# Prompt attention of a two-layer streaming encoder on Trainium2: item order, score banks, the bias pass and the place where keys are turned

## The chip, the cores and the metric

The kernel runs on one core of a Trainium2 chip. The metric is the device time of one execution in microseconds (us). Engines are called by the profile's names: PE is TensorE (matrix products; PEld its weight loads), DVE is VectorE, ACT is ScalarE, POOL is GpSimd, SP is the engine that issues most loads. Every engine works through its own list in order and waits on semaphores. PSUM is the memory that TensorE writes to: eight banks of 512 fp32 columns on 128 partitions.

## The reference

One call computes a prompt (1024 tokens of one new stream) and a sample step (16 tokens for each of 8 running streams) through two layers. Layer 0 is an mLSTM mixer and a SwiGLU FFN, layer 1 is differential attention on one shared set of keys and values, and a second FFN. The change lies in layer 1's attention of the prompt:

```
def _diff_block(q, k_all, v_all, q_pos, k_pos, rel_bias, lam):
    s = jnp.einsum('bqhjd,bkhjd->bhjqk', q, k_all).astype(jnp.float32) * (DA_DH ** -0.5)
    bias = rel_bias.astype(jnp.float32)[_t5_bucket(k_pos[None, :] - q_pos[:, None])]
    bias = bias.transpose(2, 0, 1)[None, :, None]
    mask = (k_pos[None, :] // CHUNK) <= (q_pos[:, None] // CHUNK)
    p = jax.nn.softmax(jnp.where(mask, s + bias, -jnp.inf), axis=-1)
    a = p[:, :, 0] - lam * p[:, :, 1]
    return jnp.einsum('bhqk,bkhe->bqhe', a.astype(v_all.dtype), v_all)
```

There are 8 heads. Each has two maps (j = 0, 1) of 64 dimensions and values of 128. The output of a head is normalised by its root mean square over the 128 values, scaled, and goes through the output projection. The new keys and values are outputs of the kernel too, in their natural layout (token by token).

## The kernel before, in words

All activations lie transposed in SBUF: features on partitions, the 1152 tokens (1024 prompt, 128 sample) along the row. F1 holds the queries (head h's two maps on partitions 0 to 63 and 64 to 127), F0 the keys in the same way. A projection runs in units of 128 output columns: 72 products of 128 x 384, with activations and weights each split into a high and a low half. SP loads a unit's weights into WRAW, POOL splits them into WHI and WLO, TensorE multiplies, ACT copies the finished group out of PSUM. The stages in order are: query projection `q_a`, key projection `k_a` (eight units, copied to F0), value projection `v_a` (eight units; each group is copied to VT, turned block by block by TensorE, copied to NSA and stored to the output), prompt attention, sample attention, output projection `out_a`.

Prompt attention is written out by hand as 64 items n. Item n covers query tile i = n // 8 and head h = n % 8, so tiles are outermost, and the number of keys w = 128 (i + 1) grows from 128 to 1024 over the stage. An item's work:

- `scores(n)` on TensorE: for each map the product of the query tile and w keys, in chunks of up to 512 columns. Up to 512 keys a map has two banks by turns; above that (wide items) a map has one pair of banks, and its scores wait until the exponentials of the same map of the item before are done.
- `maximum(n, j)` on DVE: adds the bias to the nearest 256 keys and takes their maximum in one pass (L1274), takes the maximum of the far keys in another (L1276), and joins the two and turns the sign (L1278).
- `exps(n, j)` on ACT: the exponential and its sum, from PSUM to one of two buffer pairs (L1154).
- `combine(n)` on DVE: two reciprocals, the factor, and one pass over w columns that joins the two maps (L1291 to L1297).
- `turn(n)` on TensorE: turns the w columns block by block into banks 4 and 5 (L1050); `copies(n)` on ACT copies them to PTS (L1163).
- `values(n)` on TensorE: the product with the values, two passes for each block of 128 keys, into bank 6 (L1063); `outs(n)` on ACT scales it into F1, and squares it for the norm (L1172, L1173).

TensorE takes, for each n, the scores of item n + 1, the turn of item n - 1 and the values of item n - 2. When a query tile's eight heads are done, POOL makes the reciprocal root (L987, L991), DVE scales the tile (L1301), TensorE turns it in two halves into bank 7 (L1040) and DVE copies it back (L1305). In the same stage the keys are turned for the output: TensorE turns half a tile into bank 7 (L1031), ACT copies it to KNAT (L1182) and issues the store, 18 times in all.

Of the kernel before, what the change touches and what calls it, by code (L numbers as in the profile page):

```python
# [18 lines left out]
ALU = mybir.AluOpType  # L19
# [3 lines left out]
P = 128  # L23
# [112 lines left out]
def build(nc, x_prompt, x_sample, state_C, state_n, state_m, cache_k, cache_v, norm_g, mlstm_w_in,  # L136
# [4 lines left out]
    with ctx, nc.allow_non_contiguous_dma(reason="a few gates, stabilisers and tables of rows"):  # L141
# [133 lines left out]
        PR = [r(f"PR{j}", [P, SEQ]) for j in range(2)]  # L275
        PR2 = [r(f"PRB{j}", [P, SEQ]) for j in range(2)]
        PTS = r("PTS", [P, SEQ // P, P])
        KNAT = r("KNAT", [P, 512])
# [592 lines left out]
        a_pt = sem("a_pt")  # L871
        a_cp = sem("a_cp")
        a_o = sem("a_o")
# [3 lines left out]
        k_tr = sem("k_tr")  # L877
        k_cp = sem("k_cp")
        k_sent = sem("k_sent")
# [22 lines left out]
        PAIRS = [PR, PR2]  # L902
        VSTORED = 16 + 32 * (UNITS["v_m"] + UNITS["v_a"])
# [7 lines left out]
        def key_tile(c):  # L911

            return 0 if c < 2 else NQ if c < 4 else c // 2 - 1

        def key_half(n):

            i, h = n // DH, n % DH
            if i < NQ and h in (0, 2):
                return h // 2 if i == 0 else 2 * i + 2 + h // 2
            if i == 0 and h in (4, 6):  # L920
                return 2 + (h - 4) // 2
            return None
# [22 lines left out]
        def attention_sp(sp):  # L945
            sp.wait_ge(nsv_sent, VSTORED)
            sp.wait_ge(group_ready, G0["out_a"])
            sp.dma_start(VP[:, 0, :], vp[:, 0, :]).then_inc(vp_first, 16)
            sp.dma_start(VP[:, 1:, :], vp[:, 1:, :]).then_inc(vp_landed, 16)
# [33 lines left out]
        def attention_pool(pool):  # L983
            for i in range(NQ):
                pool.wait_ge(a_ev, DH * (i + 1))

                pool.tensor_scalar(MSQ[:, :], SSQ[:, i % 2, :], 1.0 / P, EPS, ALU.mult, ALU.add)  # L987
                pool.drain()
                if i >= 2:
                    pool.wait_ge(a_on, i - 1)  # L990
                pool.tensor_tensor(RSTD[:, i % 2, :], MSQ[:, :], HALF[:, :], ALU.pow).then_inc(a_rstd, 1)  # L991
                pool.drain()

        def attention_pe(pe):
# [12 lines left out]
            def scores(n):  # L1007
                i, h = n // DH, n % DH
                w = (i + 1) * P
                wide = w > 512  # L1010
# [1167 lines left out]
```

## Time and profile before

| | us |
|---|---|
| median of three runs | 3546.78 |
| lowest, highest | 3543.9, 3556.37 |
| span of the profiled execution | 3551.3 |
| TensorE busy in it | 3284.0 (92%) |
| DVE, ACT, POOL busy in it | 1146.1, 726.7, 957.0 |

The span runs from the first instruction to the last one of the profiled execution. No time is given apart from it for that execution; the span lies inside the range of the three runs. The profile's busy time of TensorE counts a product from its start to its modelled end, the way through the array included, so a stretch of short dependent products looks busier than its columns are. Of the span, the prompt's attention covers about 1970 to 2292 us, and the key projection and value projection about 1753 to 1960.

### The profile page before, as it was taken

How to read it: one execution, taken by the hardware profiler on the slowest of the kernel's cores; microseconds unless marked ns; L12 is line 12 of the kernel's file. 1: busy time of each engine (PE TensorE's matmuls, PEld its weight loads, DVE VectorE, ACT ScalarE, POOL GpSimd, SP SyncE). 2: the span in 40 equal slices, each digit the busy share in tenths (PEclk: the TensorE clock that was granted, in tenths of full speed). 3: DMA queues.
4: the chain of work that ended last, by engine and by line, in shares of the span. 5: the costliest groups of instructions: out<-in, count | busy, mean ns of one | idle time of the engine just before them, and what ended most of it. 6: DMA issues, size and time to landing. Idle time of an engine off the chain costs nothing.

```text
span 3551.3 us, 45000 instructions
## 1 busy us (share of the span) xinstructions
PE 3284.0 (92%) x18277; PEld 3075.1 (87%) x18277; DVE 1146.1 (32%) x1777; ACT 726.7 (20%) x1199; POOL 957.0 (27%) x449
## 2 busy tenths in 40 slices
PE   7999987979999999988899789899879999999996
PEld 6999877969999999986899456577869999999995
DVE  5100344152222222234200677522234222222225
ACT  4111342230000000023101566411231000000002
POOL 2323001343333333323333000000243333333332
PEclk8999778989999999998999899977799999999998
DMA  4121202101111111112113210153211111111111
GB/s 146 42 83 54 84 30 94 55 24 42 42 41 41 41 41 41 41 36 77 36 42 91 97 39 22 58 178 115 78 30 32 45 42 41 41 41 41 41 42 54
DMA packets 230817, 200.87 MB, mean 57 GB/s; under 512 B 8577, under 2 KB 193310, under 8 KB 230194
## 3 DMA queue, kind: packets, MB, share of 16 engines
q1 hardware_dynamic: 194402, 147.90, 13.5%
q10 hardware_dynamic: 36304, 51.46, 4.2%
q8 instruction: 74, 1.21, 0.1%
q14 instruction: 37, 0.30, 0.0%
HBM read 166.27 MB, written 33.06 MB: 56 GB/s over the span
## 4 chain that ended last, share of the span: by engine, by line
PE 76%; issue 14%; DVE 4%; ACT 2%; POOL 1%; POOLq 1%; DVEq 1%; DMA 0%; ACTq 0%; SPq 0%
PE PS L1581 22%; PE PS L1587 22%; PE PS L1585 22%; PE PS L1127 2%; PE PS L1094 1%; DVE F L2005 1%; PE PS L1105 1%; PE PS L1128 1%; PE PS L508 1%; PE PS L485 1%; DVE F L2018 1%; DVE XLO L1989 1%; POOLq L1507 0%; PE PS L493 0%; PE PS L1117 0%
## 5 line engine op out<-in xcount | busy, mean ns | idle before, releaser
L1581 PE MATMUL PS<-XHI,WHI 128*128 128x384 f32 x3672 | 845.6, 338 | 62.7 <-DVE XLO L1989 62.4
L1506 POOL TENSOR_TENSOR WHI<-WRAW,ZERO 128x1024 fp32r<-128x1024 f32 x197 | 373.6, 1897 | 1904.9 <-PE PS L1581 1875.3
L1585 PE MATMUL PS<-XLO,WHI 128*128 128x384 f32 x3672 | 838.9, 336 | 0.0
L1587 PE MATMUL PS<-XHI,WLO 128*128 128x384 f32 x3672 | 838.6, 336 | 0.0
L1581 PEld LDWEIGHTS PS<-XHI,WHI 128*128 128x128 f32 x3672 | 656.8, 189 | 73.0 <-issue 56.0
L1585 PEld LDWEIGHTS PS<-XLO,WHI 128*128 128x128 f32 x3672 | 659.7, 189 | 0.0
L1587 PEld LDWEIGHTS PS<-XHI,WLO 128*128 128x128 f32 x3672 | 659.0, 189 | 0.0
L1508 POOL TENSOR_TENSOR WLO<-WRAW,WHI 128x1024 fp32r<-128x1024 f32 x197 | 487.5, 2474 | 28.1
L2048 DVE TENSOR_TENSOR F<-F,PS 128x1152 f32<-128x1152 f32 x176 | 238.2, 1353 | 460.4 <-PE PS L1587 460.4
L2033 DVE TENSOR_TENSOR HF<-PS,SG 128x1152 f32<-128x1152 f32 x44 | 59.7, 1357 | 668.3 <-PE PS L1587 668.3
L1863 ACT ACTIVATE HHI<-HF 128x1152 fp32r<-128x1152 f32 x44 | 51.4, 1169 | 1060.6 <-DVEq L2034 1060.6
L1581 PE MATMUL PS<-HHI,WHI 128*128 128x384 f32 x1056 | 243.5, 338 | 5.3 <-DVE HLO L2036 5.3
L1585 PE MATMUL PS<-HLO,WHI 128*128 128x384 f32 x1056 | 242.8, 338 | 0.0
L1587 PE MATMUL PS<-HHI,WLO 128*128 128x384 f32 x1056 | 242.7, 338 | 0.0
L1581 PEld LDWEIGHTS PS<-HHI,WHI 128*128 128x128 f32 x1056 | 189.7, 188 | 6.7 <-DVE HLO L2036 5.9
L1587 PEld LDWEIGHTS PS<-HHI,WLO 128*128 128x128 f32 x1056 | 190.1, 188 | 0.0
L1585 PEld LDWEIGHTS PS<-HLO,WHI 128*128 128x128 f32 x1056 | 189.9, 188 | 0.0
L2036 DVE TENSOR_TENSOR HLO<-HF,HHI 128x1152 fp32r<-128x1152 f32 x44 | 139.0, 3160 | 56.4 <-ACT HHI L1863 56.4
L1019 PE MATMUL PS<-F,F 64*128 64x512 f32 (+3 forms) x384 | 137.5, 545 | 16.1 <-ACTq L1156 12.9
L1858 ACT ACTIVATE SG<-PS 128x1152 f32<-128x1152 f32 x44 | 49.9, 1135 | 421.4 <-PE PS L1587 421.4
L1019 PEld LDWEIGHTS PS<-F,F 64*128 64x128 f32 x384 | 55.2, 200 | 73.1 <-issue 32.4
L1063 PE MATMUL PS<-VP,PTS 128*128 128x128 f32 x576 | 82.5, 291 | 23.9 <-ACTq L1175 23.9
(284 smaller groups left out, 2737.9 us busy)
## 6 DMA issues: line engine op xcount, KB each, us to landing
WRAW<-in_ffn_w_in_dram SPq DMA_DIRECT2D x88, 512.0 KB, 3.8
WRAW<-in_ffn_w_out_dram SPq DMA_DIRECT2D x44, 512.0 KB, 3.6
KC<-in_cache_k_dram SPq DMA_DIRECT2D x16, 1024.0 KB, 7.0
VC<-in_cache_v_dram SPq DMA_DIRECT2D x16, 1024.0 KB, 5.1
WRAW<-in_mlstm_w_in_dram SPq DMA_DIRECT2D x24, 512.0 KB, 3.8
xs_scratch<-F ACTq DMA_DIRECT2D x2, 4608.0 KB, 13.3
F<-xs_scratch ACTq DMA_DIRECT2D x2, 4608.0 KB, 13.9
WRAW<-in_kv_w_dram SPq DMA_DIRECT2D x16, 512.0 KB, 3.9
```

The lines of the kernel that those rows point to most:

```text
L1019: mm = pe.matmul(sflat(j, wide, n)[:, c:e], F1[64 * j:64 * j + 64, h, tile(i)], F0[64 * j:64 * j + 64, h, c:e], start=True, stop=True)
L1063: mm = pe.matmul(PS[:, 6, 0:P], PTS[:, k, :], VP[:, k, h * P:(h + 1) * P], start=k == 0, stop=k == nk - 1)
L1127: pe.matmul(out, VC[m % 4][:, t, h, :], PTC[:, t, 32 * h:32 * h + 32], start=t == 0, stop=False)
L1506: pool.tensor_tensor(WHI[par][:, :, :], WRAW[par][:, :, :], bc(bc(ZERO[:, 0], KT), P), ALU.add)
L1508: pool.tensor_tensor(WLO[par][:, :, :], WRAW[par][:, :, :], WHI[par][:, :, :].bitcast(F32), ALU.subtract).then_inc(w_split, 1)
L1581: mm = pe.matmul(out[:, c, :], wh, rhs_hi[:, chunk(c)], start=first, stop=False)
L1585: pe.matmul(out[:, c, :], wh, rhs_lo[:, chunk(c)], start=False, stop=False)
L1587: mm = pe.matmul(out[:, c, :], wl, rhs_hi[:, chunk(c)], start=False, stop=last)
L1863: act.activation(HHI[:, t, :].rearrange("p (c t) -> p c t", c=NC), HF[:, :, :], ACT.Copy).then_inc(hh_ready, 1)
L2033: dve.tensor_tensor(HF[:, :, :], G(o), SG[:, :, :], ALU.mult).then_inc(group_free[o % 2], 1)
L2036: dve.tensor_tensor(HLO[:, t, :].rearrange("p (c t) -> p c t", c=NC), HF[:, :, :], HHI[:, t, :].rearrange("p (c t) -> p c t", c=NC).bitcas ...
L2048: dve.tensor_tensor(f, f, G(o), ALU.add).then_inc(group_free[o % 2], 1)
```

## The change

- Heads are outermost: item n is head n // 8 and query tile n % 8, so every head starts with 128 keys and ends with 1024.
- The scores of all items, narrow or wide, go to three pairs of banks by turns (banks 0 to 5), item by item and map by map. Item n + 1 waits, once for both maps, for the exponentials of map 0 of item n and of map 1 of item n - 1; the two maps' chunks alternate in the list.
- Bias and maximum are one DVE pass over all w columns, with the sign turned in it. The bias stands in a row of 1024 columns for each head (BROW, two buffers that POOL fills: zeros, and the near 256 columns of a head). The exponential takes scale -1.
- Turned blocks have one bank (6). Blocks one to four are turned and copied by ACT as before; blocks five to eight are turned into the same bank after that copy and copied by DVE. Outputs go to bank 7, by turns with the turned halves of finished outputs. PTS has two buffers, the first map's exponentials three.
- A head's outputs are scaled by POOL in one pass over 1024 columns, where DVE scaled a tile.
- Keys are turned in the key projection, by the code of the value projection, with one more copy into F0. The 18 half-tile turns, copies and stores leave attention.
- The values of the first head are loaded first, where the first tile's were.

```
-        def sflat(j, wide, n):
-            if wide:
-                return PS[:, 2 * j:2 * j + 2, :].rearrange("p b c -> p (b c)")
-            return PS[:, 2 * j + n % 2, :]
+        def sflat(n, j, w):
+            b = 2 * ((2 * n + j) % 3)
+            return PS[:, b:b + 2, :].rearrange("p b c -> p (b c)")[:, 0:w]
...
         def attention_pool(pool):
+            def bias_rows(h):
+                if h >= 2:
+                    pool.wait_ge(a_m[0], NQ * (h - 1))
+                    pool.wait_ge(a_m[1], NQ * (h - 1))
+                pool.tensor_copy(BROW[h % 2][:, SEQ - NEAR:], BIAS[:, h, :]).then_inc(bias_row, 1)
+            pool.wait_ge(group_ready, G0["out_a"])
+            for j in range(2):
+                pool.memset(BROW[j][:, 0:SEQ - NEAR], 0.0)
+            pool.drain()
+            pool.wait_ge(lam_dve, 1)
+            bias_rows(0)
+            bias_rows(1)
+            for h in range(DH):
+                pool.wait_ge(a_ev, NQ * (h + 1))
...
+                o = F1[:, h, 0:SEQ].rearrange("p (i e) -> p i e", i=NQ)
+                pool.tensor_tensor(o, o, bc(RSTD[:, h % 2, :], P), ALU.mult).then_inc(a_on, 1)
...
             def scores(n):
-                for j in range(2):
-                    back = 1 if wide else 2
-                    if n >= back:
-                        pe.wait_ge(a_e[j], n - back + 1)
-                    for c in range(0, w, 512):
+                if n >= 1:
+                    pe.wait_ge(a_e[0], n)
+                if n >= 2:
+                    pe.wait_ge(a_e[1], n - 1)
+                for c in range(0, w, 512):
+                    e = min(c + 512, w)
+                    for j in range(2):
...
+            def turn(n, second):
+                nk = n % NQ + 1
+                if second:
+                    if not wide(n):
+                        return
+                    pe.wait_ge(a_cp, n + 1)
+                    ks_ = range(4, nk)
+                else:
+                    pe.wait_ge(a_c, n + 1)
+                    if n:
+                        pe.wait_ge(a_cp, n)
+                        pe.wait_ge(a_cpb, wides(n - 1))
+                    ks_ = range(min(nk, 4))
...
             for n in range(NI + 2):
                 if n + 1 < NI:
                     scores(n + 1)
+                if n < NI and out_turn(n) is not None:
+                    pe.wait_ge(a_ev, n - 2)
+                    out_half(out_turn(n))
+                    turned = out_turn(n) + 1
                 if 1 <= n <= NI:
-                    turn(n - 1)
+                    turn(n - 1, False)
                 if n >= 2:
-                    values(n - 2)
+                    values(n - 2, turned)
+                if 1 <= n <= NI:
+                    turn(n - 1, True)
...
             act.wait_ge(nsv_sent, VSTORED)
+            act.wait_ge(w_split, U0["out_a"] + 3)
...
+            exps(0, 0)
             for n in range(NI + 3):
                 if n < NI:
                     exps(n, 1)
                 if n >= 3:
                     outs(n - 3)
+                if 1 <= n <= NI:
+                    copies(n - 1)
+                if n + 1 < NI:
+                    exps(n + 1, 0)
...
             def maximum(n, j):
-                dve.tensor_tensor_reduce(near, near, bias, 1.0, -3e38, ALU.add, ALU.max, stat(n, j))
-                if far:
-                    dve.tensor_reduce(stat(n, 2 + j), s[:, 0:far], AX_X, ALU.max)
+                dve.tensor_tensor_reduce(s, s, BROW[h % 2][:, SEQ - w:], -1.0, 3e38, ALU.add, ALU.min, stat(n, 4 + j))
+                dve.drain().then_inc(a_m[j], 1)
...
-            linear("k_a", 4)
-            values("v_a", UNITS["v_m"])
+            values("k_a", UNITS["v_m"], 4)
+            values("v_a", UNITS["v_m"] + UNITS["k_a"])
```

TensorE's list in attention, before, at two items of 768 keys, one with a half of turned outputs (L1019 scores, L1040 turned outputs, L1050 turn, L1063 values; PR and PRB are the two buffer pairs of exponentials):

```order
L1019 MATMUL PS<-F_49,F_50 128x512 [waits a_e0]
L1019 MATMUL PS<-F_49,F_50 128x256
L1019 MATMUL PS<-F_49,F_50 128x512 [waits a_e1]
L1019 MATMUL PS<-F_49,F_50 128x256
L1040 MATMUL PS<-CST,F_50 128x128 [waits k_cp,a_on]
L1040 MATMUL PS<-CST,F_50 128x128 x3
L1050 MATMUL PS<-CST,PRB_145 128x128 [waits a_cp,a_c]
L1050 MATMUL PS<-CST,PRB_145 128x128 x5
L1063 MATMUL PS<-VP,PTS 128x128 [waits a_ev,a_cp]
L1063 MATMUL PS<-VP,PTS 128x128 x5
```

TensorE's list in attention, after, from the second to the fourth tile's scores of a head, with the wide tiles of the head before among them (L1036 scores, L1066 turn, L1082 values; P is an item's first map's buffer):

```order
L1036 MATMUL PS<-F_49,F_50 128x256 [waits a_e1,a_e0]
L1036 MATMUL PS<-F_49,F_50 128x256
L1066 MATMUL PS<-CST,P_143 128x128 [waits a_cpb,a_cp,a_c]
L1066 MATMUL PS<-CST,P_143 128x128 x3
L1082 MATMUL PS<-VP,PTS_147 128x128 [waits a_ev,o_cp,a_cpb,a_cp]
L1082 MATMUL PS<-VP,PTS_147 128x128 x6
L1066 MATMUL PS<-CST,P_143 128x128 [waits a_cp]
L1066 MATMUL PS<-CST,P_143 128x128 x3
L1036 MATMUL PS<-F_49,F_50 128x384 [waits a_e1,a_e0]
L1036 MATMUL PS<-F_49,F_50 128x384
L1066 MATMUL PS<-CST,P_144 128x128 [waits a_cpb,a_cp,a_c]
```

The two maps' scores now follow one another behind one common wait, the turn is in two parts around the values, and the turn also waits for DVE's copies (`a_cpb`); the scores of narrow tiles stand behind the turns and values of the last head's wide tiles.

DVE's list in attention, before, one step of the tile of 512 keys (two maxima, then the combination of the item before):

```order
L1274 ISA PS,ST<-PS,BIAS 128x256 [waits a_c,a_s0]
L1274 ISA ST 128x1
L1276 TENSOR_REDUCE ST<-PS 128x1
L1278 SCALAR_TENSOR_TENSOR ST<-ST,NEG 128x1
L1274 ISA PS,ST<-PS,BIAS 128x256 [waits a_c,a_s1]
L1274 ISA ST 128x1
L1276 TENSOR_REDUCE ST<-PS 128x1
L1278 SCALAR_TENSOR_TENSOR ST<-ST,NEG 128x1
L1291 RECIPROCAL ST<-ST 128x1 [waits a_ev,a_e1,a_e0]
L1292 RECIPROCAL RL_139<-ST 128x1
L1294 SCALAR_TENSOR_TENSOR ST<-ST,LAM 128x1
L1297 SCALAR_TENSOR_TENSOR PRB_145<-PRB_146,ST,PRB_145 128x512
```

DVE's list in attention, after, at the tile of 896 keys, with a half of turned outputs (L1313), the combination of the item of 768 keys and the copy of the item of 640 keys (L1308):

```order
L1285 ISA PS,ST<-PS,BROW_150 128x896 [waits a_e0,a_s0,bias_row]
L1285 ISA ST 128x1
L1313 TENSOR_SCALAR F_50<-PS,LAM 128x512 [waits o_tr]
L1285 ISA PS,ST<-PS,BROW_150 128x896 [waits a_e1,a_s1,bias_row]
L1285 ISA ST 128x1
L1295 RECIPROCAL ST<-ST 128x1 [waits a_ev,a_e1,a_e0]
L1296 RECIPROCAL RL_139<-ST 128x1
L1298 SCALAR_TENSOR_TENSOR ST<-ST,LAM 128x1
L1301 SCALAR_TENSOR_TENSOR P_144<-P_146,ST,P_144 128x768
L1308 COPY PTS_147<-PS 128x128 [waits a_o,a_ptb]
```

Each map has one pass in place of three instructions, and the copy of turned blocks stands at the end of the step.

## Rows read from the trace of the kernel before

**Rows 1.** Windows: length; busy (count) PE, PEld, DVE, ACT, POOL; clock; DMA share; GB/s.

```profile
1973.00:2010.00 37.00, 25.18 (x102) 17.02 (x102) 24.82 (x127) 24.38 (x93) 1.85 (x2) 0.59 0.30 117
2013.00:2068.00 55.00, 41.37 (x232) 24.82 (x232) 46.59 (x191) 41.73 (x132) 3.67 (x4) 0.97 0.17 58
2068.00:2272.00 204.00, 190.59 (x967) 122.03 (x965) 148.81 (x430) 125.60 (x286) 7.33 (x8) 1.00 0.06 22
```

**Rows 2.** Groups by shape, prompt attention: count, busy, mean ns, idle before.

```profile
L1274 DVE CUSTOM_DVE_ANT_0 PS<-PS,BIAS 128x256 f32<-128x256 f32 x112 | 48.3, 431 | 49.5 <-PE PS L1019 47.7 <-DVE PRB L1297 0.5
L1154 ACT ACTIVATE PR<-PS,ST 128x512 f32<-128x512 f32 x8 | 5.5, 685 | 1.6 <-DVE ST L1278 1.2 <-issue 0.3
L1305 DVE TENSOR_SCALAR F<-PS,LAM 128x512 f32<-128x512 f32 x15 | 11.2, 745 | 1.2 <-PE PS L1040 1.2
L1274 DVE CUSTOM_DVE_ANT_0 PS<-PS,BIAS 128x128 f32<-128x128 f32 x16 | 4.8, 299 | 4.4 <-PE PS L1019 3.8
L1297 DVE SCALAR_TENSOR_TENSOR PR<-PR,ST,PR 128x128 f32<-128x128 f32 x4 | 1.4, 352 | 0.3
```

**Rows 3.** Timeline of a step of 768 keys: start, length, engine, [idle before].

```profile
2150.58 0.89 ACT L1154 ACTIVATE PRB<-PS,ST 128x768 f32<-128x768 f32 x1
2151.64 1.55 PE L1019 MATMUL PS<-F,F 64*128 64x512 f32 x4 [0.38 <-ACTq L1156]
2151.65 0.14 DVE L1274 DVE_READ_ACCUMULATOR2_ANT ST<- 128x1 f32 x1
2153.84 1.50 PE L1063 MATMUL PS<-VP,PTS 128*128 128x128 f32 x12
2154.48 0.16 DVE L1291 RECIPROCAL ST<-ST 128x1 f32<-128x1 f32 x1
2155.07 1.02 DVE L1297 SCALAR_TENSOR_TENSOR PRB<-PRB,ST,PRB 128x768 f32<-128x768 f32 x1
```

**Rows 4.** Timeline, TensorE, scores of an item of 512 keys, both maps.

```profile
2069.09 1.13 PE L1019 MATMUL PS<-F,F 64*128 64x512 f32 x4
```

**Rows 5.** Timeline, ACT and TensorE: last key unit, last value units.

```profile
1853.25 1.13 ACT L1830 ACTIVATE F<-PS 128x1152 f32 x1 [11.35 <-PE PS L1587]
1946.49 1.13 ACT L1838 ACTIVATE RS<-PS 128x1152 f32<-128x1152 f32 x1 [2.84 <-PE PS L1587]
1959.97 1.13 ACT L1838 ACTIVATE RS<-PS 128x1152 f32<-128x1152 f32 x1 [2.85 <-PE PS L1587]
1961.15 1.09 PE L1644 MATMUL PS<-CST,RS 128*128 128x128 f32 x8 [1.22 <-ACT RS L1838]
1963.42 0.33 PE L1649 MATMUL PS<-CST,RS 128*128 128x128 f32 x1 [1.17 <-ACT NSA L1842]
```

**Rows 6.** Timeline, first maximum and the end of prompt attention.

```profile
1973.27 0.30 DVE L1274 CUSTOM_DVE_ANT_0 PS<-PS,BIAS 128x128 f32<-128x128 f32 x1
2286.40 0.20 POOL L987 TENSOR_SCALAR MSQ<-SSQ 128x8 f32<-128x8 f32 x1 [48.55 <-ACTq L1175]
2288.41 1.23 DVE L1301 TENSOR_TENSOR F<-F,RSTD 128x1024 f32<-128x1024 f32 x1 [14.40 <-POOL RSTD L991]
2292.41 1.72 PEld L1094 LDWEIGHTS PS<-CST,KC 128*128 128x128 f32 x8
```

**Rows 7.** DVE and POOL side by side: two lines' durations (min/median/max) and timelines.

```profile
L2005 DVE SCALAR_TENSOR_TENSOR F<-F,GALL,RS x24: 1417/1419/3784, 710.1 to 2649.2; 128x1152 f32<-128x1152 f32 x24
L1506 POOL TENSOR_TENSOR WHI<-WRAW,ZERO x197: 1892/1892/2370, 10.3 to 3473.2; 128x1024 fp32r<-128x1024 f32 x197
713.12 3.67 POOL L1524 TENSOR_TENSOR F<-F,F 128x1152 f32<-128x1152 f32 x1 [17.20 <-DVE F L2005]
714.23 5.27 DVE L2005 SCALAR_TENSOR_TENSOR F<-F,GALL,RS 128x1152 f32<-128x1152 f32 x2
2005.32 1.65 POOL L991 TENSOR_TENSOR RSTD<-MSQ,HALF 128x8 f32<-128x8 f32 x1
2006.16 0.48 DVE L1297 SCALAR_TENSOR_TENSOR PR<-PR,ST,PR 128x256 f32<-128x256 f32 x1
```

More of the change, by code:

```diff
@@ L1023, in keys @@
-            def keys(c):
-                i, half = key_tile(c), c % 2
+                if n >= 1:
[5 more added lines that the diff above has]
+                    for j in range(2):
+                        mm = pe.matmul(sflat(n, j, w)[:, c:e], F1[64 * j:64 * j + 64, h, tile(i)],
+                                       F0[64 * j:64 * j + 64, h, c:e], start=True, stop=True)
+                        if e == w:
+                            mm.then_inc(a_s[j], 1)
@@ L1026, in keys, with out_half @@
+            def out_half(c):
+                h, half = c // 2, c % 2
+                pe.wait_ge(a_on, h + 1)
                 if c:
-                    pe.wait_ge(k_cp, c)
-                if 1 < i < NQ and not half:
-                    pe.wait_ge(o_cp, 2 * i - 2)
+                    pe.wait_ge(o_cp, c)
                 for k in range(4):
-                    mm = pe.transpose(PS[:, 7, k * P:(k + 1) * P], F0[:, 4 * half + k, tile(i)], ident)
-                mm.then_inc(k_tr, 1)
-            def out_half(i, half):
-                pe.wait_ge(a_on, i + 1)
-                pe.wait_ge(k_cp, min(2 * i + 6, 2 * NT))
-                if half:
-                    pe.wait_ge(o_cp, 2 * i + 1)
-                for k in range(4):
-                    mm = pe.transpose(PS[:, 7, k * P:(k + 1) * P], F1[:, 4 * half + k, tile(i)], ident)
-                mm.then_inc(o_tr, 1)
@@ L1043, in turn @@
-            def turn(n):
-                nk = n // DH + 1
-                pe.wait_ge(a_c, n + 1)
-                if n:
-                    pe.wait_ge(a_cp, n)
-                for k in range(nk):
-                    mm = pe.transpose(PS[:, 4 + k // 4, (k % 4) * P:(k % 4 + 1) * P], PAIRS[n % 2][0][:, tile(k)], ident)
-                mm.then_inc(a_pt, 1)
-            def values(n):
-                h, nk = n % DH, n // DH + 1
+                    mm = pe.transpose(PS[:, 7, k * P:(k + 1) * P], F1[:, h, tile(4 * half + k)], ident)
@@ new lines, in out_half @@
+                mm.then_inc(o_tr, 1)
+            def turn(n, second):
[11 more added lines that the diff above has]
+                    ks_ = range(min(nk, 4))
+                for k in ks_:
+                    mm = pe.transpose(PS[:, 6, (k % 4) * P:(k % 4 + 1) * P], P0[n % 3][:, tile(k)], ident)
+                mm.then_inc(a_ptb if second else a_pt, 1)
@@ L1175, in outs @@
[L1175 to L1185 removed]
+                if i == 0 and h >= 2:
+                    act.wait_ge(a_rstd, h - 1)
@@ L1633, in linear, with values @@
                     two(i, 0, None)
-            def values(name, first):
+            def values(name, first, split=None):
                 u0, o0 = U0[name], G0[name]
@@ L1649, in turn_last, with unit @@
                     pe.transpose(PS[:, 6, 0:P], VT[:, tile(NT - 1)], ident).then_inc(nt_tr, 1)
-                def unit(j, i, turns):
+                def unit(j, i, turns, split=None):
                     o = o0 + j
@@ L1837, in values @@
                         act.wait_ge(group_ready, o0 + j + 1 + 2 * i)
+                        if kept is not None:
+                            out = kept[:, bass.ds(j + 2 * i, 1), :].rearrange("p a (c t) -> p (a c) t", c=NC)
+                            act.activation(out, G(o0 + j), ACT.Copy)
                         act.activation(VT[:, :].rearrange("p (c t) -> p c t", c=NC), G(o0 + j), ACT.Copy
```

193 lines of the change are left out of this document (84 added, 109 removed).

## Prediction

> **What bounds the kernel now.** I read the stages' windows first, then the groups by shape, then single steps of the timeline. Prompt attention is 64 items (8 heads x 8 query tiles; an item of tile i scores w = 128(i+1) keys in two maps). It begins with DVE's first maximum at 1973.27 and ends when TensorE turns to the sample's keys at 2292.41 [rows 6]: 319.1 us. TensorE is busy 93% of its wide part (tiles of 640 to 1024 keys), 75% before that, 68% in the first 37 us, where the granted clock is 0.59, about its lower level of 1.2 GHz [rows 1]. In wide items each map has its own wait, so TensorE does them one after the other: 1.55 us for one map of 768 keys, as two passes of 512 and two of 256 columns [rows 3]. In narrow items both maps are ready together, and their four passes of 512 columns take 1.13 us [rows 4]; one after the other, at 0.42 for the two passes of 256 (1.55 - 1.13 leaves that), they would need about twice as long. So the wide part is bound by TensorE's serial scores; what the change has to win lies there.
>
> **Keys turned in the key projection.** 18 half-tiles of four turns, 18 evacuations and their stores leave attention; a turn, its evacuations and stores follow each of the eight units of the key projection. The value projection already does exactly this, and both are visible: a plain unit takes 1.13 + 11.35 = 12.48 us, a unit with turns 1959.97 - 1946.49 = 13.48 [rows 5]: 7 x 1.0 = 7.0 us. The eighth unit's turns stand bare: from the end of its products (1959.97) to the last turn (1963.42 + 0.11) 3.6 us, and the change puts a second copy of 1.13 us ahead of that chain: 4.7. Together **11.7 us added**, all on TensorE's path. The copies and stores hide under the 12.5 us of a unit; ACT issues the stores, with no load of weights queued behind them (those are SP's). Were that cover gone, one unit's copies (about 3.6 us) would show.
>
> **The new step, by engine.** An item's DVE pass now takes bias and maximum over all w columns. The old pass took 431 ns at 256 and 299 at 128 columns [rows 2], so 1.03 ns a column: 0.70, 0.96, 1.22 us at 512, 768, 1024; a maximum with read-out and drain costs M = pass + 0.13. A combination takes 0.59 before its wide pass, which is 0.35 at 128 and 1.02 at 768 columns [rows 2, 3]. New on DVE is the copy of turned blocks five to eight, priced by the nearest pass from PSUM, 0.745 for 512 columns [rows 2]: 0.3 to 0.75, in all 2.2 a head; two halves of outputs are 1.6 with gaps. A head has 36 blocks of 128 keys, 4608 columns a map. DVE's work in it is then 16 maxima, 2 x (8 x 0.17 + 4.61 x 1.03 + 8 x 0.13) = 14.3, + 8 combinations, 8 x 0.64 + 6.5 = 11.6, + 2.2 + 1.6 = **29.7 us**. TensorE's own is 36 x (0.21 for the scores of both maps side by side, 0.11 for a turn, 0.22 for two passes of values) + 0.9 = 20.5, plus some 3 of fill. ACT, busy 76% and 62% in the two later windows [rows 1], loses the copies of blocks five to eight and the keys. So DVE takes over as the bound.
>
> **What the order adds.** Scores of item n+1 wait for the first map's exponentials of item n, so a step cannot be shorter than M + E + S: maximum, exponential until TensorE starts (2151.64 - 2150.58 = 1.06 at 768 [rows 3], by the 685 ns row 0.85 at 512), scores (1.13 at 512 [rows 4], 0.21 per further 128). From 512 to 640 keys that is 0.83 + 0.85 + 1.34 = 3.0 against 2.9 of DVE work; then 3.5 against 3.3, and 3.9 against 3.7: with the step before them 0.6 in a head. At a head's start TensorE still owes the wide tiles of the last head: 14 and 16 passes of values at 0.112 (twelve in 1.50 [rows 3]) and up to 8 turns at 0.11 [rows 5], queued ahead of the scores of tiles 2 and 3, and the turn now waits for DVE's copy of the item before, because one bank serves all turned blocks. Laying these in order by hand, tiles 1 and 2 take 3.6 and 3.15 us where DVE has 2.9 and 2.5 of work: 1.4. So a head takes 29.7 + 0.6 + 1.4 = **31.7 us**, or 4.0 an item, where the old items took 299/64 = 4.7 or so (from 1973.3 to about 14 us before the last output at 2286.4 [rows 6]).
>
> **POOL's multiplication.** Normalising a head's outputs moves from DVE (1.23, [rows 6]) to POOL. POOL takes 1.89 for 1024 columns with a broadcast operand [rows 7]; nothing shows this very form, so 1.9 to 3.7 bound it and I take 1.9, the nearest. It starts about 2 us (0.20 + 1.65 and waits) after a head's last output, into the next head's third or fourth combination. Two rows show what that does: beside POOL's sum of two tiles a DVE pass over SBUF operands that takes 1.42 alone took 3.78 [rows 7]. I take 1.3 of waiting in each of seven heads (0 to 1.9): 9.1. The small power operation did nothing of the kind: a combination of 0.48 lay wholly inside its 1.65 [rows 2, 7]. The Trainium skill, in "SBUF — State Buffer" (Who interferes with whom), says that a DVE instruction with two SBUF inputs contends with any GpSimd instruction that reads SBUF, and that the loser waits for the whole instruction. By it the power operation would stall a combination too, some 1 us more in seven heads, and the sum would come to 3530. The trace shows that it did not, so it is left out.
>
> **Cheap parts.** POOL clears the bias rows after the last value unit and copies the first one when DVE has lambda's sums, shortly before its first maximum at 1973.27 [rows 6]: the copy is a quarter of 1.89, 0.5, and would cost that once if it came late. POOL's later bias rows (six) are a quarter of a tile each and needed a head later. ACT's new wait on the output projection's first weights is met long before; behind POOL's list only the second output weights queue, needed 200 us later. SP's value load is the same size, first head first; TensorE waits for the rest only at item 8.
>
> **The sum.** Steps: 8 x 31.7 = 253.6, + 9.1 for POOL, + 6 for one more wait per maximum and short spells of lower clock (0 to 12, taken in the middle), - 1 as the first head owes nothing: 267.7. From 1973.3 that is 2241.0. The last item's combination, copies, turn and values take 9.7; then POOL's 2.0 + 1.9 and two output halves 1.9 [rows 6]: 15.5, so 2256.5 against 2292.4: 35.9 us gained, less 11.7: **24 us**. The profiled execution's span is 3551.3, 4.5 above the median of the runs; I take the difference from the median: 3546.8 - 24 = **3523 us**.
>
> **Rivals.**
> - *DVE's floor.* Loop, order and POOL cost nothing: 8 x 29.7 = 238, some 28 less with POOL's 9 and half the small terms: 3495. For it: slack between narrow and wide items; against it: every exponential of map 0 stands behind the copy of the turned block on ACT.
> - *Twice the loss.* Waits on three engines, or a POOL pass of 3.7, cost 2 us a head more than laid out: 16, so 3539, no change. For it: the old kernel's steps already show many small idles (0.4 before a wide score [rows 3]).
> - *The maps don't run side by side in wide items*, where each has two chunks; no row shows that form. Then scores of 640 to 896 keys take up to 1.3 longer in the loop, 3 a head: 24, so 3547, no change. Against it: [rows 4].
> - *Slower by the clock.* Each head now begins with narrow items. In the first 37 us, where all items were narrow, the granted clock was 0.59; from 2013 on, with 256 to 512 keys, 0.97 [rows 1]. If the thin stretch of every head (tiles 1 to 5) ran at 1.2 GHz, the scores in the loop would cost 0.64 + 0.85 + 1.07 + 1.28 = 3.8 more and the owed values and turns 2.5: 6.3 a head, 50 in all: 3573. It eats the gain from four heads in eight on. Against it: the owed wide work fills the narrow items.
>
> **How the numbers follow.** Forecast 0.47, floor 0.14, twice the loss 0.20, maps apart 0.08, clock 0.11. The likeliest has 3523. The range goes from the floor, 3496, to 3555, part of the way to the clock's case; beyond it lies about 0.2. A difference of 0.5% (17.7 us) is about what a measurement can tell. Faster takes the floor and nine tenths of the forecast, 0.56; same the rest of it, twice the loss and maps apart, 0.33; slower the clock, 0.11.
>
> **What would show it.** Right: in each wide item two maps' passes start within 10 ns; DVE busy above 85% of attention and first on its chain; heads 31 to 34 us apart; units of the key projection 13.5 us. POOL's multiplication: one combination a head 1 to 2 us longer than its width says. Wrong: granted clock well under 1 in the middle of attention; heads beyond 36 us; or heads under 30, with DVE never idle.

## The result, and the profile after

| | before | after |
|---|---|---|
| time, median of 9 runs each | 3552.2 us | 3558.5 us |
| ratio, 95% interval | | 1.0027 [1.0019, 1.0035] |
| profiled execution, span | 3551.3 us | 3555.0 us |
| prompt attention, first maximum to the sample's keys | 319.1 us | 311.8 us |

By the medians the kernel became 6 us slower; the ratio, which is reckoned from all runs and is not the quotient of the two medians, puts it at 7 to 12. A gain of 24 us was forecast, and the time lies just above the range's upper end of 3555. In the two traces the difference of 3.7 us has four parts. Key and value projections take 14.6 us more (first key evacuation to first maximum: 207.4 us before, 222.0 after). Prompt attention takes 7.3 us less instead of 35.9. What follows it takes 2.9 more; no run here asks why. And 6.5 us less were spent long before the changed stages: from 375 to 405 us the profiled execution of the kernel before ran 30.7 us at a granted clock of 0.5 and the one after 13.7. That is chance: the first key evacuation comes at 1765.88 in the one and 1759.41 in the other, and kernels of the experiments show both (1760.13 in the one with pieces, 1766.04 in the one with pieces and no bare tail).

Key projection, timeline of after: two units, 13.47 apart, then the last unit and the start of the value projection.

```profile
1800.88 1.13 ACT L1846 ACTIVATE RS<-PS 128x1152 f32<-128x1152 f32 x1
1814.35 1.13 ACT L1846 ACTIVATE RS<-PS 128x1152 f32<-128x1152 f32 x1
...
1854.79 1.13 ACT L1846 ACTIVATE RS<-PS 128x1152 f32<-128x1152 f32 x1
1855.97 1.50 PE L1649 MATMUL PS<-CST,RS 128*128 128x128 f32 x8 [2.35 <-ACT RS L1846]
1858.65 0.48 PE L1654 MATMUL PS<-CST,RS 128*128 128x128 f32 x1 [1.18 <-ACT NSA L1850]
1858.78 1.31 PE L1586 MATMUL PS<-XHI,WHI 128*128 128x384 f32 x3
1859.88 1.16 PE L1590 MATMUL PS<-XLO,WHI 128*128 128x384 f32 x3
1863.55 0.69 PE L1592 MATMUL PS<-XHI,WLO 128*128 128x384 f32 x3
```

Windows of after (columns as in [rows 1]): the bare tail (the last key unit's turns, which no product covers) and what follows it, a run of steady heads, then one head cut where the clock changes.

```profile
1850.00:1857.00 7.00, 4.65 (x29) 4.30 (x28) 0.00 (x0) 2.43 (x3) 0.00 (x0) 0.96 0.30 87
1857.00:1864.00 7.00, 5.82 (x22) 5.42 (x21) 0.00 (x0) 1.30 (x2) 4.26 (x2) 0.55 0.28 84
...
2057.00:2245.00 188.00, 144.67 (x824) 100.24 (x822) 137.55 (x351) 113.83 (x322) 22.46 (x20) 0.86 0.07 23
...
2132.00:2143.00 11.00, 7.74 (x50) 4.90 (x47) 8.53 (x22) 7.02 (x23) 4.49 (x4) 1.00 0.30 96
2143.00:2147.00 4.00, 3.56 (x13) 1.89 (x14) 2.10 (x7) 1.97 (x7) 0.00 (x0) 0.57 0.00 0
2147.00:2160.00 13.00, 9.20 (x60) 5.89 (x59) 10.83 (x26) 9.47 (x21) 0.00 (x0) 1.00 0.01 2
2160.00:2167.00 7.00, 5.87 (x25) 5.16 (x27) 4.51 (x12) 3.01 (x13) 0.00 (x0) 0.52 0.00 0
```

In the middle of attention (2057 to 2245) the granted clock is 0.86, where the wide part before had 1.00 [rows 1], and no engine is the bound: TensorE is busy 77%, VectorE 73%. Steady heads, those behind the second, are 37.55 us apart, all alike but for 0.1, against 33.0 in the forecast (31.7 and 1.3 for POOL). Each contains two stretches at 1.2 GHz, of 3.4 and 6.8 us. Here is the place before the first, in the timeline of after:

```profile
2138.55 1.35 PE L1036 MATMUL PS<-F,F 64*128 64x512 f32 x8 [1.13 <-ACTq L1181]
2138.85 1.90 POOL L1008 TENSOR_TENSOR F<-F,RSTD 128x1024 f32<-128x1024 f32 x1 [0.16 <-issue]
2138.93 0.14 DVE L1296 RECIPROCAL RL<-ST 128x1 f32<-128x1 f32 x1
2139.16 1.60 DVE L1298 SCALAR_TENSOR_TENSOR ST<-ST,LAM 128x1 f32<-128x1 f32 x1
2140.84 0.62 DVE L1301 SCALAR_TENSOR_TENSOR P<-P,ST,P 128x384 f32<-128x384 f32 x1
2141.51 0.55 PE L1066 MATMUL PS<-CST,P 128*128 128x128 f32 x3 [1.61 <-DVE P L1301]
2141.90 0.61 PE L1082 MATMUL PS<-VP,PTS 128*128 128x128 f32 x4
2143.44 2.93 PE L1036 MATMUL PS<-F,F 64*128 64x512 f32 x8 [0.93 <-ACTq L1181]
```

POOL's multiplication holds up an operation on one column (L1298, 0.22 us elsewhere) to its own end. The combination behind it is late, TensorE idles 1.61 ahead of the turn and 0.93 ahead of the scores, and those scores, 768 keys of both maps, run at 1.2 GHz: 2.93 us. (My expectations below call them the scores of 640 keys; those are the 1.35 above.) And this stands before and in the second stretch:

```profile
2158.68 0.49 PE L1036 MATMUL PS<-F,F 64*128 64x128 f32 x4 [0.84 <-ACTq L1181]
2161.05 1.11 PE L1048 MATMUL PS<-CST,F 128*128 128x128 f32 x4 [1.88 <-ACTq L1199]
2161.96 1.06 PE L1066 MATMUL PS<-CST,P 128*128 128x128 f32 x4
2163.10 2.90 PE L1082 MATMUL PS<-VP,PTS 128*128 128x128 f32 x12
2165.79 0.85 PE L1066 MATMUL PS<-CST,P 128*128 128x128 f32 x3
2166.57 0.95 PE L1036 MATMUL PS<-F,F 64*128 64x256 f32 x4
```

Behind the last wide scores of a head come those of one block (0.49), and the output half then waits 1.88 for ScalarE's evacuation. What follows runs at 1.2 GHz. Twelve passes of values take 2.90; before they took 1.50 [rows 3].

### The profile page after: what moved, and what is told of

Read it like the earlier page. It is cut to its first block, busy times and chain, and to the rows that moved or that the text cites. A ratio compares the mean times of both kernels' runs of the same rounds, so it can differ in the third digit from the quotient of the medians.

```text
span 3555.0 us, 45098 instructions
## 1 busy us (share of the span) xinstructions
PE 3251.0 (91%) x18277; PEld 3064.4 (86%) x18277; DVE 1138.4 (32%) x1577; ACT 730.3 (21%) x1205; POOL 979.4 (28%) x467
## 4 chain that ended last, share of the span: by engine, by line
PE 81%; DVE 7%; issue 5%; ACT 2%; POOL 1%; DVEq 1%; POOLq 1%; ACTq 1%; DMA 0%; SPq 0%
PE PS L1586 22%; PE PS L1590 22%; PE PS L1592 22%; PE PS L1149 2%; PE PS L1036 2%; PE PS L1082 2%; DVE PS L1285 1%; PE PS L1116 1%; DVE F L2013 1%; PE PS L1066 1%; PE PS L1127 1%; PE PS L1150 1%; PE PS L510 1%; PE PS L1649 1%; PE PS L487 1%
## 5 line engine op out<-in xcount | busy, mean ns | idle before, releaser
L1036 PE MATMUL PS<-F,F 64*128 64x512 f32 (+3 forms) x384 | 94.3, 602 | 38.3 <-ACTq L1181 35.2
L1285 DVE CUSTOM_DVE_ANT_0 PS<-PS,BROW 128x256 f32<-128x256 f32 (+7 forms) x128 | 97.8, 764 | 39.6 <-PE PS L1036 22.8
L2003 DVE SCALAR_TENSOR_TENSOR XN<-F,GALL,RS 128x1152 f32<-128x1152 f32 x40 | 58.6, 1466 | 128.4 <-PE PS L1592 86.4
## 6 DMA issues: line engine op xcount, KB each, us to landing
F<-xs_scratch ACTq DMA_DIRECT2D x2, 4608.0 KB, 13.7
```

Of the source, the lines that this page charges most:

```text
L1036: mm = pe.matmul(sflat(n, j, w)[:, c:e], F1[64 * j:64 * j + 64, h, tile(i)], F0[64 * j:64 * j + 64, h, c:e], start=True, stop=True)
L1285: dve.tensor_tensor_reduce(s, s, BROW[h % 2][:, SEQ - w:], -1.0, 3e38, ALU.add, ALU.min, stat(n, 4 + j))
```

## The experiments

All ratios are against the kernel before, measured beside each run. "After" is the changed kernel, at 1.0027. Where a difference from after is given in us, it is one of medians from different sessions; by the ratios such a gain is up to 2.3 us smaller.

**Tiles alternating.**

```
+        ORDER = (4, 3, 5, 2, 6, 1, 7, 0)
...
-            return n // NQ, n % NQ
+            return n // NQ, ORDER[n % NQ]
```

> The changed kernel with one edit: within a head the tiles run in the order 4, 3, 5, 2, 6, 1, 7, 0, so that wide and narrow items alternate; work, waits, banks and the places of the output halves stay. Theory 'clock' (the thin run of tiles 1 to 4 and the idle ahead of the second output half let the granted clock fall twice a head, about 10 of 37.5 us): granted clock 0.97 or more in the attention windows against 0.85, heads 31 to 34 us apart instead of 37.55, 25 to 45 us faster than the changed kernel, so about 3515 to 3533. Theory 'waits' (the three engines wait for one another item by item, and the clock falls only because TensorE waits): the sum of an head's steps stays, heads 36 us or more, within 10 us of the changed kernel.

Measured: 1.0025 [1.0016, 1.0035], 3557.1 us. The alternation did not hold the clock, so by its time the run fits theory 'waits' as it was put, but it does not tell the two apart. One head of the profiled execution, however, happened to keep the clock; windows of four heads:

```profile
2068.93:2106.68 37.75, 29.12 (x166) 21.27 (x168) 25.85 (x71) 22.64 (x65) 4.88 (x4) 0.86 0.08 29
2106.68:2144.33 37.65, 29.02 (x166) 20.26 (x168) 25.84 (x70) 22.61 (x65) 4.88 (x4) 0.86 0.10 29
2144.33:2178.07 33.74, 24.93 (x166) 17.14 (x168) 25.84 (x71) 22.58 (x65) 4.89 (x4) 1.00 0.09 32
2178.07:2215.99 37.92, 29.01 (x166) 20.28 (x168) 27.37 (x71) 22.57 (x65) 4.59 (x4) 0.86 0.08 29
```

The same instructions take 33.74 us at 1.00 and 37.7 at 0.86, with VectorE equally busy (25.84) in the first three: 3.9 us a head are the clock's. (In the fourth, VectorE waits for POOL as well: a combination of 768 keys, 1.02 elsewhere, takes 2.55 at 2186.18.) My edit missed; the head that kept the clock bears the theory out.

**The output half behind the turn.**

```
+                if 1 <= n <= NI:
+                    turn(n - 1, False)
                 if n < NI and out_turn(n) is not None:
                     pe.wait_ge(a_ev, n - 2)
                     out_half(out_turn(n))
                     turned = out_turn(n) + 1
-                if 1 <= n <= NI:
-                    turn(n - 1, False)
```

> The changed kernel with one edit: on TensorE the half of outputs of the head before is turned behind the item's first turn instead of ahead of it, so that the turn no longer stands behind the wait for the last evacuated output. Theory 'waits': the turn of steps 5 and 7 starts about 1.1 us earlier each (2151.53 against a combination that ended 2150.50; 2161.96 against 2160.85), the loop gets this back: 1.5 to 2.3 us a head in seven heads, 10 to 16 us faster than the changed kernel. Theory 'clock': the idle of TensorE is the same length, only in another place; the granted clock stays at 0.85, and the time moves by less than 6 us.

Measured: 1.0037 [1.0022, 1.0051], 3560.6 us, no gain, as theory 'clock' expected. The values now wait for VectorE's read of the half (0.94 and 1.09 us in one head), and clock stretches stay (steady heads 36.9 to 38.6).

**TensorE kept busy, heavily and lightly.**

```
-                for k in range(nk):
+                for k in list(range(nk)) * (8, 5, 4, 3, 2, 2, 1, 1)[nk - 1]:   # lightly: (5, 3, 2, 1, 1, 1, 1, 1)
```

> The changed kernel with one edit: TensorE repeats the values' products of the narrow items (8, 5, 4, 3, 2, 2 times for 1 to 6 blocks, same operands and target, so the same result) in places where it stood idle for 0.7 to 1.1 us. Theory 'clock': granted clock rises from 0.85 to 0.95 or more in the attention windows, the scores of 640 keys take 1.4 us instead of 2.9, heads 33 to 35.5 us apart, 15 to 35 us faster than the changed kernel although 4 us of work a head are added. Theory 'waits': the added work lies on TensorE's path or in its idle: no change to 2 us a head slower, 0 to 16 us slower.

> The changed kernel with a lighter filling of TensorE: values' products repeated for items of 1, 2 and 3 blocks only (5, 3, 2 times: 22 passes of 0.11, 2.4 us a head, each behind a turn and ahead of an idle of 0.9 to 1.1 us). Theory 'clock': the first fall of each head (3.4 us, in which the scores of 640 keys take 2.9 instead of 1.4) goes, the second (6.8 us, behind the idle ahead of the second output half) stays: time at the lower level in attention from 97 to about 70 us, 6 to 14 us faster than the changed kernel. Theory 'waits': not faster, up to 10 us slower.

Measured: heavily 1.0076 [1.0060, 1.0093], 3575.8 us, slower; lightly 0.9981 [0.9971, 0.9991], 3541.4 us, 17 us faster than after, although 2.4 us of useless work a head were added. The heavy one held the clock (33.6 us of attention at the lower level instead of 97) but I had sized it wrongly: a block is two passes, so it added 9.6 us a head, not 4, and much of that stood on the path: a head that keeps a clock of 1.00 takes 38.76 there (2062.71 to 2101.47). The light one is the clean test, and gained more than the 6 to 14 us expected. In the heads of its profile one or two stretches of 3.4 us are left by turns:

```profile
2056.23:2091.21 34.98, 28.73 (x189) 20.77 (x187) 27.53 (x70) 22.66 (x65) 4.49 (x4) 0.95 0.09 31
2091.21:2127.95 36.74, 29.99 (x189) 22.25 (x187) 27.13 (x71) 22.71 (x65) 4.49 (x4) 0.91 0.08 29
2127.95:2162.91 34.96, 28.72 (x189) 20.78 (x187) 27.51 (x71) 22.62 (x65) 4.49 (x4) 0.95 0.10 31
2162.91:2199.64 36.73, 30.00 (x189) 22.25 (x187) 27.48 (x71) 22.71 (x65) 4.49 (x4) 0.91 0.09 29
```

One stretch of 3.4 us costs 1.77 us of a head here.

**POOL's multiplication left out, and cut into pieces.** In the first, outputs of the prompt are not normalised; the second's edit is shown.

```
-                pool.tensor_tensor(o, o, bc(RSTD[:, h % 2, :], P), ALU.mult).then_inc(a_on, 1)
+                for k in range(NQ):
+                    op = pool.tensor_tensor(o[:, k:k + 1, :], o[:, k:k + 1, :], bc(RSTD[:, h % 2, k:k + 1], P), ALU.mult)
+                op.then_inc(a_on, 1)
```

> The changed kernel without POOL's multiplication of a head's outputs by the reciprocal root mean square (it is left out, nobody else does it; the rest, with the power operation, stays). If the multiplication costs only what its neighbour on VectorE waits (a tiny operation of 0.22 us that takes 1.60 beside it): 1.4 us a head, 8 to 12 us faster than the changed kernel, granted clock 0.85 to 0.87 as before. If this wait is also what leaves TensorE idle long enough for the first fall of the clock in each head, the scores of 640 keys go from 2.9 to 1.4 us as well: 20 to 30 us faster, clock 0.90 or more.

> The changed kernel with POOL's multiplication of a head's outputs cut into 8 instructions of 128 columns. VectorE's small operation (0.22 alone, 1.60 beside the whole multiplication) can then wait for one piece only, an eighth of 1.89 or about 0.3 us. Theory 'the wait for the whole instruction, and the fall of the clock behind it, cost the 27 us that leaving the multiplication out gave': nearly all of it comes back here, 18 to 26 us faster than the changed kernel, heads about 34.3 us apart, scores of 640 keys 1.4 us instead of 2.9. Rival 'what costs is POOL's traffic itself, whatever its pieces': several operations wait one after another, less than 10 us faster.

Measured: without it 0.9955 [0.9938, 0.9972], 3531.4 us; in pieces 0.9964 [0.9952, 0.9977], 3534.6 us. The time at the lower level in attention falls from 97 to 51 and 55 us, and heads are about 34 us apart in both. A steady head keeps 3.4 us of lower clock out of 10.2: the first stretch is gone, and half of the second. Timeline with pieces:

```profile
2096.37 3.21 POOL L1009 TENSOR_TENSOR F<-F,RSTD 128x128 f32<-128x128 f32 x8 [0.16 <-issue]
2097.09 0.40 DVE L1300 SCALAR_TENSOR_TENSOR ST<-ST,LAM 128x1 f32<-128x1 f32 x1
2097.58 0.68 DVE L1303 SCALAR_TENSOR_TENSOR P<-P,ST,P 128x384 f32<-128x384 f32 x1
2100.23 1.56 PE L1038 MATMUL PS<-F,F 64*128 64x512 f32 x8 [0.93 <-ACTq L1183]
```

POOL takes longer in all (3.21 against 1.90), VectorE waits 0.2 instead of 1.4, and the scores of 768 keys are back at 1.56. So the wait and the clock behind it together cost 24 of the 27 us (22 of 26 by the ratios); POOL's traffic as such costs little.

**One part alone: keys turned in the key projection, in the kernel before; with the bare tail and without.** The second moves the last key unit's turns behind the first products of the value projection (`lead`: the first unit, too, turns what came before it).

```
-            linear("k_a", 4)
-            values("v_a", UNITS["v_m"])
+            values("k_a", UNITS["v_m"], 4)              # second kernel: last=False
+            values("v_a", UNITS["v_m"] + UNITS["k_a"])  # second kernel: lead=True
```

> The kernel before with one part of the change alone: keys are turned and stored in the key projection; its attention keeps its order, banks and passes and loses the key halves. The key projection should end 14.5 us later than in the kernel before, as in the changed kernel (7 for seven units, 4.7 for the bare tail, the rest the clock behind the tail). In attention 18 times four turns (7.9 us of TensorE) and as many evacuations (12 us of ACT) go; if TensorE was the bound there, attention is 8 to 12 us shorter and the kernel 3 to 7 us slower than before; if the key halves lay in idle time, attention is under 4 us shorter and the kernel 10 to 15 us slower.

> The kernel before with keys turned and stored in the key projection and the last unit's turns behind the first products of the value projection, so without the bare tail; its attention as it was, without the key halves. Turning the keys there alone came out even with the kernel before; without the tail it should be 6 to 7.5 us faster than before: 3540 to 3542, ratio 0.998.

Measured: 0.9997 [0.9987, 1.0006], 3547.7 us; without the tail 0.9981 [0.9971, 0.9990], 3541.2 us. Attention got 14.7 us shorter (1988.12 to 2292.55: 304.4; 306.0 in the second kernel), more than I expected, and this pays for the projection. So the rest of the change, banks, passes and order together, made attention 6 to 7 us longer (304.4 or 306.0 to 311.8).

**Pieces and no bare tail; outputs evacuated early at the halves; filling again.** Each run keeps the edits of the one ahead of it. The second:

```
+                early = n % NQ in (5, 7)
+                if n >= 3 and early:
+                    outs(n - 3)
                 if n < NI:
                     exps(n, 1)
-                if n >= 3:
+                if n >= 3 and not early:
                     outs(n - 3)
```

> The changed kernel with the multiplication in pieces and the last key unit's turns moved behind the first products of the value projection's first unit, so that no turn of keys stands bare. If the bare tail costs 4.7 us and the half clock behind it 2.8, it is 7.5 us faster than the pieces alone, about 3527, and the key projection's end stands 7 us, not 14.5, behind that of the kernel before. If the clock falls there for another reason: 4 to 5 us.

> The kernel of the run before (pieces, no bare tail) with one more edit: in the two steps with an output half ScalarE evacuates the last outputs ahead of the second map's exponentials, so that TensorE's half no longer waits for both (in the kernel without the multiplication it idles 1.9 us, 2149.37 to 2151.24, and turns, with the half ahead, 0.7 us after the combination is ready). Theory 'the wait ahead of the half, and the clock's fall behind it, make up most of the 2.3 us a head by which heads stay above my step sum': heads 34.0 to 32 us, time at the lower level from 55 to about 30 us, 12 to 18 us faster than the run before. Rival, as moving the half behind the turn showed: the step is set by exponentials and scores in any case, within 5 us.

> The kernel of the run before last edit kept (pieces, no bare tail, outputs early at the halves), with TensorE's values' products repeated in part for the items of 1, 2, 3 and 5 blocks (4, 3, 3 and 3 blocks more, 0.22 us each: 2.9 us a head, in idles of 0.9 to 1.1 us). There the lower level still takes one stretch of 3.4 us a head, over the twelve passes of values of tile 5. Theory 'clock': without it these passes take 1.4 instead of 2.5 us, the scores and turns behind them 0.5 less: heads 34.1 to 32.5 us, 8 to 14 us faster than the run without the repeats. Theory 'my step sum is short': the clock holds and heads stay at 33.5 to 34.5, or the clock isn't held: within 4 us, or slower by the added work.

Measured: 0.9943 [0.9926, 0.9959], 3528.0 us; 0.9940 [0.9920, 0.9960], 3526.2 us; 0.9929 [0.9913, 0.9946], 3523.6 us. Without the bare tail 6.6 us came back. The early outputs cut TensorE's idle ahead of the half from 1.88 to 0.33, but the turn then waits for VectorE, and the stretch of 3.4 us a head stayed, in the third kernel too: heads 34.1 to 34.4 in both. My two expectations of 12 to 18 and 8 to 14 us missed (2 and 3 us came).

**Another order of the same work**, values ahead of the turn. Two more edits went with it: VectorE's copies of blocks five to eight ahead of the second maximum, and ScalarE's outputs ahead of the exponentials.

```
+                halves = n < NI and out_turn(n) is not None
+                if n >= 2 and not halves:
+                    values(n - 2, turned)
+                if 1 <= n <= NI:
+                    turn(n - 1, False)
+                if halves:
                     pe.wait_ge(a_ev, n - 2)
...
```

> The changed kernel with another order of the same work: TensorE forms the values of item n-2 ahead of the turn of item n-1 (except in the two steps with an output half, where the half and the values follow the turn), VectorE copies blocks five to eight between the two maxima instead of behind the combination, ScalarE evacuates outputs ahead of the second map's exponentials. Theory 'loop': the path from a combination over turn, copy, first exponential to the next scores carries values and waits that my step sum left out, 1 to 2 us in the wide steps; they leave it: 2 to 3 us a head, 14 to 24 us faster than the changed kernel, more if TensorE's idle and with it the clock's falls shrink. Theory 'POOL and clock alone': VectorE's wait of 1.4 and the half clock stay, under 6 us faster.

Measured: 1.0130 [1.0111, 1.0149], 3596.8 us, a miss on the other side: heads of 41.6 us and more. In the steps with a half a circle of waits arose. VectorE, timeline:

```profile
2180.14 0.75 DVE L1315 TENSOR_SCALAR F<-PS,LAM 128x512 f32<-128x512 f32 x1
2182.31 0.29 DVE L1310 COPY PTS<-PS 128x128 f32<-128x128 f32 x1 [1.42 <-PE PS L1066]
2182.52 1.09 DVE L1287 CUSTOM_DVE_ANT_0 PS<-PS,BROW 128x896 f32<-128x896 f32 x1
```

The copy that I had put ahead of the second maximum waits for turns that TensorE makes behind values, which wait for VectorE's read of the half (L1315): 1.42 us, with the second maximum queued behind. This accounts for part of the 4 us a head; the rest was not taken apart.

**A head that begins with a wider tile.**

```
+        ORDER = (3, 2, 1, 0, 4, 5, 6, 7)    # the other kernel: (2, 1, 0, 3, 4, 5, 6, 7)
```

> The kernel with pieces, no bare tail and outputs early at the halves, with the tiles of a head in the order 3, 2, 1, 0, 4, 5, 6, 7. The scores behind those of tile 7 are then 512 columns wide (1.13 us against 0.49), where TensorE idled 1.2 us ahead of the turn and the clock fell behind it. Theory 'clock': no stretch at 1.2 GHz in a steady head, heads 32 to 33 us apart instead of 34.1, 8 to 16 us faster than with the tiles in order. Theory 'step sum short': heads 33.7 us or more whatever the clock, within 4 us.

> The same with the order 2, 1, 0, 3, 4, 5, 6, 7: scores of 384 columns (0.9 us) behind those of tile 7. Theory 'clock': the stretch goes or is halved, heads 32.3 to 33.5 us; the one- and two-block items then stand inside the head, and a new stretch there would show as scores of 640 keys at 2.9 us and take the gain back. Theory 'step sum short': heads 33.7 us or more, within 4 us of the tiles in order.

Measured: from tile 3 on 0.9917 [0.9900, 0.9933], 3517.2 us; from tile 2 on 0.9932 [0.9916, 0.9949], 3522.9 us, with heads of 32.9 to 34.4. Windows of five heads, from tile 3 on:

```profile
2048.12:2082.03 33.91, 26.48 (x166) 17.99 (x164) 26.19 (x71) 22.56 (x66) 5.13 (x11) 0.95 0.10 32
2082.03:2115.77 33.74, 26.32 (x166) 17.87 (x164) 26.18 (x71) 22.40 (x65) 5.13 (x11) 0.95 0.10 33
2115.77:2148.16 32.39, 24.67 (x164) 16.68 (x163) 26.00 (x70) 22.19 (x65) 5.13 (x11) 1.00 0.10 33
2148.16:2180.56 32.40, 24.98 (x167) 17.00 (x165) 26.05 (x70) 22.50 (x65) 5.13 (x11) 1.00 0.10 34
2180.56:2212.95 32.39, 24.98 (x167) 17.00 (x165) 26.15 (x70) 22.50 (x65) 5.13 (x11) 1.00 0.01 2
```

Three heads, the first two of these among them, have one stretch of 3.4 us (from 2041.8, 2076.0, 2110.1), the steady ones behind them none. The same head takes 33.8 with it and 32.4 without, and 32.4 is 0.7 above my step sum of 31.7. This kernel, changed in four places, beats both: 31 us faster than before, 41 faster than after (39 by the ratio). Against the kernel before with its keys turned early and no bare tail (3541.2) it is 24 us faster: with the clock mostly held, order, banks and passes do pay.

## Why the prediction was wrong, point by point

**Key projection.** Units are 13.47 us apart: right, as the value units of [rows 5] had shown. The bare tail was counted (4.7); what was left out is that TensorE, idle for 2.35 and 1.18 in it, begins the value projection at a granted clock of 0.55 (0.69 us for three passes become 1.16). The part cost 14.6 instead of 11.7; without the bare tail it is 8.0 (first key evacuation to first maximum 215.4 against 207.4).

**What leaves attention with the keys.** I gave it no price of its own, since VectorE was to be the bound. Alone it was worth 13 to 14.7 us, so on balance this part cost nothing; the gain that I expected from banks, passes and order was a loss of 6 to 7.

**Engines.** Durations were right: maxima of 0.70, 0.97 and 1.23 us at 512, 768 and 1024 columns, the copy of 512 columns 0.69. The maps do run side by side in wide items: their passes start 7 ns apart, with 1.99 us for 1024 keys of both maps in after (2153.93), 1.56 for 768 in the kernel with pieces, against 1.55 for one map before [rows 3]. That rival is out. "VectorE above 85% busy" was wrong (73%), and even in the best kernel it is 80% (78.2 of 97.2 us, in the three heads at full clock): no single engine sets the steps, but waits among three, and the clock. Two slips in the prediction change nothing: TensorE's own work is 20.3 by its terms, not 20.5, and the floor stands there as 3495 and as 3496.

**Step sum.** 31.7 was short by 0.7: the three heads at full clock, 32.4. Their tiles stand in another order, so this is near, not exact. No run reached the floor of 29.7.

**POOL's multiplication.** The wait itself was priced well: 1.0 to 1.4 in each of seven heads, 8.8 us in all against 9.1. Some of that is luck: I had expected it on the wide pass, and it fell on the operation on one column, whose duration nobody would suspect. What failed is that I stopped there. The idle that it opens on TensorE is followed by a stretch at 1.2 GHz over the widest work near, and with it the multiplication cost 27 us. The Trainium skill, in "SBUF — State Buffer" (Who interferes with whom), has the rule for the wait: VectorE with two SBUF inputs and a POOL instruction that reads SBUF exclude each other, and who comes second waits for the whole instruction. These traces agree for the multiplication in both directions: in three heads of the kernel with alternating tiles the combination came first, and it is POOL that took 2.65 to 2.66 instead of 1.90. For the small power operation the rule does not hold here, as it did not before the change: the operation on one column took 0.22 inside a power operation of 1.64. Timeline of one such head:

```profile
2112.83 1.64 POOL L1007 TENSOR_TENSOR RSTD<-MSQ,HALF 128x8 f32<-128x8 f32 x1
2114.21 0.22 DVE L1300 SCALAR_TENSOR_TENSOR ST<-ST,LAM 128x1 f32<-128x1 f32 x1
2114.51 1.02 DVE L1303 SCALAR_TENSOR_TENSOR P<-P,ST,P 128x768 f32<-128x768 f32 x1
2114.62 2.66 POOL L1010 TENSOR_TENSOR F<-F,RSTD 128x1024 f32<-128x1024 f32 x1 [0.16 <-issue]
```

**Clock: the rival with 0.11 had the cause, but not the places.** Both signs of being wrong that the prediction named are there: a granted clock of 0.86 in the middle of attention, and heads beyond 36 us. I had the rival as 6.3 us a head over tiles 1 to 5; it is two shorter stretches. The first lies among the wide items, behind POOL's wait. The second does lie at a head's narrow start, behind the one-block scores and the wait of 1.88; that these two bring it about is only partly shown, since cutting the wait to 0.33 left a stretch of 3.4, and wider scores in that place ended it in some heads and not in others. By rows, 768 keys cost 1.37 more (2.93 against 1.56) and the second stretch 2.8: 0.45, 0.43, 1.32, 0.36 and 0.25 in the last five rows shown of it, against the same instructions at full clock in the kernel from tile 3 on (the fifth takes 0.70, at 2148.64):

```profile
2139.75 0.66 PE L1052 MATMUL PS<-CST,F 128*128 128x128 f32 x4
2141.31 0.63 PE L1070 MATMUL PS<-CST,P 128*128 128x128 f32 x4 [0.90 <-DVE PTS L1315]
2142.85 1.58 PE L1086 MATMUL PS<-VP,PTS 128*128 128x128 f32 x12 [0.91 <-DVE F L1320]
2144.26 0.49 PE L1070 MATMUL PS<-CST,P 128*128 128x128 f32 x3
```

That is up to 4.2 us of a head; the alternating kernel shows 3.9 for its own stretches. My argument against the rival, that the owed wide work fills the narrow items, looked at the amount of work in a head's first steps and not at the idles between: behind the owed 14 and 16 passes the clock is indeed 1.00; it falls ahead of them.

**The sum.** Steady heads: 33.0 forecast, 37.55 measured. Of the 4.55, about 3.9 are the clock and 0.7 the step sum, each measured in a kernel with another order of tiles. So the step that failed is the term "one more wait per maximum and short spells of lower clock", taken at 6 us for the whole of attention (0 to 12): the clock alone took about 3.9 in a steady head, some 27 in the seven heads behind the first. Attention fell 28.6 us short of its gain, and the projection came out 2.9 over. The pieces and the missing tail, which take away 6.8 of a head's 10.2 us at the lower clock and the tail's, give 3528; that this is near the forecast's 3523 says nothing for the forecast, which was for another kernel.

Open: why one stretch stays in some heads of the kernel from tile 3 on and not in others, with the same instructions and the same idles ahead of it (0.47, 0.90 and 0.91, from 2071.05 and from 2138.69); and what the in-order tiles take at full clock, since no run of mine showed that without added work.

## What to carry to other kernels

Price a wait not only by its length but by what TensorE does behind it: here a wait of 1.0 to 1.4 us a head on VectorE cost three times as much (27 against 8.8 in all), since TensorE ran behind it at half the clock. Read the granted clock in windows cut at the period of the loop, and compare periods of one trace that differ in the clock alone; that gives its price without an experiment. Cut long POOL instructions over SBUF that run beside a chain of small VectorE operations, and put a stage's last turns behind the next stage's first products.

## What the runs showed of the hardware

The time of a one-column operation rose sevenfold (0.22 to 1.60) beside POOL's multiplication, while reciprocals of one operand next to it (L1296, 0.14) ran on undisturbed. POOL's copy of a bias row took 0.76 when it fell beside a combination (2140.95 in after) and 0.40 beside a maximum (2099.79 with pieces). Redundant passes made a kernel faster: 2.4 us of useless products a head, 17 us less in all.
